# Expert weights of a mixture-of-experts layer: six transfers of 2 MB per expert in place of twelve of 1 MB

## The reference

```
xn = rmsnorm(h)                                  # 1024 x 1024
top-4 of 32 experts per token, softmax gates
per expert e, in blocks of 128 tokens:
    gu = xb @ w_gu[e] + b_gu[e]                  # 1024 -> 2048: g, u
    h  = (clip(u) + 1) * (min(g, 7) * sigmoid(1.702 * min(g, 7)))
    yb = h @ w_down[e] + b_down[e]               # 1024 -> 1024
h = h + sum over the token's 4 experts of gate * y
out = rmsnorm_final(h)
```

## Time and profile before

| | |
|---|---|
| time, median of 3 runs | 2607.06 us (2603.6 to 2607.36) |
| profiled execution | 2609.65 us, its span 2608.0 us |
| TensorE busy | 2352.2 us (90%) |
| VectorE busy | 1590.6 us (61%) |
| ScalarE busy | 1117.3 us (43%) |
| moved by DMA | 514.21 MB |
| expert weight transfers | 256 of w_gu and 128 of w_down, 1 MB each |
| item loop | from about 990 us to about 2518 us |

### The profile page before, as it was taken

The page is one execution under the profiler, slowest core; times in us unless marked ns, Lnnn a source line. Parts: engine busy times, 40 slices in busy tenths (PEclk is TensorE's granted clock), DMA queues, the critical chain, the costliest instruction groups (busy, mean ns, idle before and its releaser), DMA issues.

```text
span 2608.0 us, 31503 instructions
## 1 busy us (share of the span) xinstructions
PE 2352.2 (90%) x9494; PEld 1711.6 (66%) x9495; DVE 1590.6 (61%) x1522; ACT 1117.3 (43%) x1047; POOL 350.5 (13%) x338
## 2 busy tenths in 40 slices
PE   7997499989999956999999999999999999999960
PEld 4553374554554525888888888888888787778840
DVE  4446841110131366786876666787778779978748
ACT  4123120030130213565654544556566567765632
POOL 0370300000000052010110100111011011110016
PEclk9989659989999957999999999999999999999985
DMA  4002010130100116786876866778789789997857
GB/s 151 33 1 83 1 81 33 35 126 29 36 19 1 67 66 235 289 302 222 327 268 225 290 224 211 281 278 324 254 313 369 247 313 370 371 338 267 313 209 289
DMA packets 215265, 514.21 MB, mean 197 GB/s; under 512 B 19140, under 2 KB 19338, under 8 KB 214520
## 3 DMA queue, kind: packets, MB, share of 16 engines
q1 hardware_dynamic: 194912, 450.72, 48.5%
q0 software_dynamic: 18352, 62.60, 6.4%
q10 hardware_dynamic: 1960, 0.35, 0.1%
HBM read 481.97 MB, written 30.48 MB: 196 GB/s over the span
## 4 chain that ended last, share of the span: by engine, by line
PE 44%; issue 5%; DVE 5%; DMA 5%; ACT 2%; POOL 1%; DVEq 1%; ACTq 0%; POOLq 0%; SPq 0%
PE PS L839 17%; PE PS L860 10%; PE PS L843 9%; PE PS L867 5%; DVE WL L1602 2%; DMA WA<-in_exp_w_down 2%; DMA WA<-in_exp_w_gu 2%; PE PS L892 1%; PE PS L831 1%; DVE H L1212 1%; PE PS L804 1%; POOL WA L1884 1%; ACT WH L1112 1%; ACT WH L1117 1%; DVE XEL L1598 0%
## 5 line engine op out<-in xcount | busy, mean ns | idle before, releaser
L1602 DVE TENSOR_TENSOR WL<-WA,WH 128x2048 fp32r<-128x2048 f32 x384 | 876.6, 2290 | 288.4 <-ACT WH L1133 117.8
L839 PE MATMUL PS<-WH,XEL 128*128 128x512 f32 x1344 | 361.1, 391 | 0.0
L839 PE MATMUL PS<-WH,XEH 128*128 128x512 f32 x1344 | 360.7, 390 | 0.0
L843 PE MATMUL PS<-WL,XEH 128*128 128x512 f32 x1344 | 347.6, 390 | 0.0
L1117 ACT CAST WH<-WA 128x2048 fp32r<-128x2048 f32 x128 | 243.9, 1908 | 201.8 <-PE PS L843 150.5
L1112 ACT CAST WH<-WA 128x2048 fp32r<-128x2048 f32 x128 | 244.5, 1910 | 190.4 <-PE PS L843 155.0
L1133 ACT CAST WH<-WA 128x2048 fp32r<-128x2048 f32 x124 | 236.5, 1909 | 199.3 <-PE PS L867 181.8
L839 PEld LDWEIGHTS PS<-WH,XEL 128*128 128x128 f32 x1344 | 253.2, 188 | 53.3
L843 PEld LDWEIGHTS PS<-WL,XEH 128*128 128x128 f32 x1344 | 253.2, 188 | 52.9
L839 PEld LDWEIGHTS PS<-WH,XEH 128*128 128x128 f32 x1344 | 253.1, 188 | 52.1
L538 PE MATMUL PS<-XT,WB 128*128 128x512 f32 x512 | 223.2, 597 | 1.1 <-issue 1.1
(11 more groups left out here) (249 smaller groups left out, 2373.4 us busy)
## 6 DMA issues: line engine op xcount, KB each, us to landing
WA<-in_exp_w_gu SPq DMA_DIRECT2D x256, 1024.0 KB, 6.4
WA<-in_exp_w_down SPq DMA_DIRECT2D x128, 1024.0 KB, 6.1
y_rows<-WA POOLq DMA_DIRECT2D x42, 512.0 KB, 6.7
WB<-in_xa_wkv SPq DMA_DIRECT2D x4, 2048.0 KB, 8.0
WB<-in_w_in SPq DMA_DIRECT2D x3, 2048.0 KB, 10.4
H<-in_x SPq DMA_DIRECT2D x4, 1024.0 KB, 5.9
WB<-in_w_out SPq DMA_DIRECT2D x2, 2048.0 KB, 7.8
WA<-in_x SPq DMA_DIRECT2D x1, 4096.0 KB, 12.2
```

What stands on the lines that cost most here:

```text
L839: nc.tensor.matmul(PS[:, 2 * h + t, :], x[:, KT4 * half + k, t * P:(t + 1) * P], WH[:, j % 4, k * HALF:(k + 1) * HALF], start=False, stop= ...
L843: ins = nc.tensor.matmul(PS[:, 2 * h + t, :], XEH[:, KT4 * half + k, t * P:(t + 1) * P], WL[:, j % 4, k * HALF:(k + 1) * HALF], start=Fals ...
L1602: v.tensor_tensor(WL[:, s, :], RAW[:, s, :], WH[:, s, :].bitcast(F32), sub).then_inc(done, 1)
```

## The change

The slots of the raw ring are filled in pairs: slots 0 and 1 by one transfer of 2 MB, slots 2 and 3 by another. SP waits for the second slot of the pair to be free, instead of each in turn, and the landing semaphores are one per pair, so ScalarE may start on either slot only when both have landed. The conversion by ScalarE and VectorE stays one slot at a time, as do WH, WL and TensorE's work. The pieces within a transfer keep their form: 2 KB contiguous for gate/up, 4 KB for down.

```diff
-            for j in range(4):
-                load_gate_up(j, slice(0, 1))
+            for u in range(2):
+                load_gate_up(u, slice(0, 1))
...
+            def load_gate_up(u, e):
                 f, h = divmod(u, 2)
+                b = u % 2
+                sp.dma_start(RAW[:, 2 * b:2 * b + 2, :].rearrange("p j (k c) -> p (j k) c", k=KT4),
+                             gu_v[:, e, :, h, f, :].rearrange("p e k c -> p (e k) c")).then_inc(rg_in[b], 16)
+
+            def load_down(b, e):
+                sp.dma_start(RAW[:, 2 * b:2 * b + 2, :].rearrange("p j (k d) -> p (j k) d", k=2),
+                             dn_v[:, e, b, :, :].rearrange("p e k d -> p (e k) d")).then_inc(rd_in[b], 16)
...
-                    for s in range(4):
-                        sp.wait_ge(gu_low, 8 * i + s + 1)
-                        load_gate_up(4 + s, bass.ds(e_i, 1))
+                    for b in range(2):
+                        sp.wait_ge(gu_low, 8 * i + 2 * b + 2)
+                        load_gate_up(2 + b, bass.ds(e_i, 1))
...
-                            sp.wait_ge(gu_low, 8 * i + m + 5)
-                            load_down(m, bass.ds(e_p, 1))
+                            sp.wait_ge(gu_low, 8 * i + 2 * b + 6)
+                            load_down(b, bass.ds(e_p, 1))
...
-                            sp.wait_ge(dn_low, 4 * i + s + 5)
-                            load_gate_up(s, bass.ds(e_n, 1))
+                            sp.wait_ge(dn_low, 4 * i + 2 * b + 6)
+                            load_gate_up(b, bass.ds(e_n, 1))
...
-                    act.wait_ge(rg_in[s], 32 * i + 32)
+                    act.wait_ge(rg_in[s // 2], 32 * i + 32)
...
-                    act.wait_ge(rd_in[m], 16 * i)
+                    act.wait_ge(rd_in[m // 2], 16 * i)
...
-                    act.wait_ge(rg_in[s], 32 * i + 48)
+                    act.wait_ge(rg_in[s // 2], 32 * i + 48)
```

More of the change, by code:

```diff
@@ L323, in build @@
         bdn_in, tri_done, fg_in, h3_done = sem("bdn_in"), sem("tri_done"), sem("fg_in"), sem("h3_done")
-        rg_in = [sem(f"raw{s}_gu_in") for s in range(4)]
-        rd_in = [sem(f"raw{s}_dn_in") for s in range(4)]
+        rg_in = [sem(f"raw_pair{s}_gu_in") for s in range(2)]
+        rd_in = [sem(f"raw_pair{s}_dn_in") for s in range(2)]
         gu_high, gu_low, gu_used = sem("gu_high"), sem("gu_low"), sem("gu_used")
@@ L455, in _ @@
             sp.dma_start(BDN[0:E, :], A["exp_b_down"]).then_inc(bdn_in, 16)
[L456 to L461, removed]
+            gu_v = A["exp_w_gu"].rearrange("e (k p) (h f c) -> p e k h f c", p=P, h=2, f=2)
+            dn_v = A["exp_w_down"].rearrange("e (m k p) d -> p e m k d", p=P, k=4)
+            def load_gate_up(u, e):
                 f, h = divmod(u, 2)
[L463 to L469, removed]
+                b = u % 2
[4 more added lines that the diff above has]
+                             dn_v[:, e, b, :, :].rearrange("p e k d -> p (e k) d")).then_inc(rd_in[b], 16)
             wait_filled(sp, ("xt3", L - 1, 1))
             sp.wait_ge(xn_out, 16 * L)
-            for j in range(4):
-                load_gate_up(j, slice(0, 1))
+            for u in range(2):
+                load_gate_up(u, slice(0, 1))
             sp.wait_ge(itm_done, 1)
@@ L487, in _ @@
                     e_i = item_expert(sp, i)
-                    for s in range(4):
-                        sp.wait_ge(gu_low, 8 * i + s + 1)
-                        load_gate_up(4 + s, bass.ds(e_i, 1))
+                    for b in range(2):
+                        sp.wait_ge(gu_low, 8 * i + 2 * b + 2)
+                        load_gate_up(2 + b, bass.ds(e_i, 1))
                 with sp.If_cmp(n_p, 0, "IS_GT"):
                     e_p = entry(sp, 0, i, E - 1)
-                    for m in range(4):
+                    for b in range(2):
                         with sp.If_cmp(n_i, 0, "IS_GT"):
-                            sp.wait_ge(gu_low, 8 * i + m + 5)
-                            load_down(m, bass.ds(e_p, 1))
+                            sp.wait_ge(gu_low, 8 * i + 2 * b + 6)
+                            load_down(b, bass.ds(e_p, 1))
                         with sp.Else():
-                            sp.wait_ge(dn_low, 4 * i + m + 1)
-                            load_down(m, bass.ds(e_p, 1))
+                            sp.wait_ge(dn_low, 4 * i + 2 * b + 2)
+                            load_down(b, bass.ds(e_p, 1))
                 with sp.If_cmp(n_n, 0, "IS_GT"):
@@ L502, in _ @@
                     with sp.If_cmp(n_p, 0, "IS_GT"):
-                        for s in range(4):
-                            sp.wait_ge(dn_low, 4 * i + s + 5)
-                            load_gate_up(s, bass.ds(e_n, 1))
+                        for b in range(2):
+                            sp.wait_ge(dn_low, 4 * i + 2 * b + 6)
+                            load_gate_up(b, bass.ds(e_n, 1))
                     with sp.Else():
-                        for s in range(4):
-                            sp.wait_ge(gu_low, 8 * i + s + 5)
-                            load_gate_up(s, bass.ds(e_n, 1))
+                        for b in range(2):
+                            sp.wait_ge(gu_low, 8 * i + 2 * b + 6)
+                            load_gate_up(b, bass.ds(e_n, 1))
             sp.wait_ge(moe_done, 1)
@@ L1095, in _ @@
             for j in range(4):
-                act.wait_ge(rg_in[j], 16)
+                act.wait_ge(rg_in[j // 2], 16)
                 nc.scalar.copy(WH[:, j, :], RAW[:, j, :]).then_inc(gu_high, 1)
```

## The result

The changed kernel takes 2808.98 us (median of 4, 2802.27 to 2809.98) against 2607.21 before: a ratio of 1.077, 95% interval 1.075 to 1.079. The forecast was 2743 us in a range of 2680 to 2830: slower, as forecast, but by 202 us in place of 136.

The account below looks back on a forecast made before the run. TensorE bounds two-tile turns; in one-tile turns TensorE, VectorE and DMA are about equal and the raw ring has no slack. One-tile stretches lose 157 us, less 21 already lost: +136 on the profiled 2609.65, so 2743 us, range 2680 to 2830.

Parts of the forecast that it names:

- The ring as the bound of one-tile turns: Raw ring of two pairs: a round of 16.1 us, 48.4 us a one-tile turn where TensorE needs 35.3; chance 0.65.
- TensorE's waits: In the one-tile stretch after the change, TensorE was to wait for VectorE's difference at L1602.
- T: Landing time of a 2 MB transfer into the raw ring: 8.6 us, bounds 7.6 and 9.9.
- Two-tile turns hide it: With two tiles the flow takes 4.2 us per slot against TensorE's 5.88, so TensorE stays the bound and turns are unchanged.
- The stock: Slots ready behind a two-tile stretch: eight, worth 8.7 us in one-tile slots; four two-tile slots give 6.7 back.
- Larger transfers are cheaper: Rival: DMA pays its fixed part half as often, one-tile turns fall to TensorE's 35.3 us, total 2586 us; chance 0.04.
- Hidden by the stock: Rival: slots in stock hide the delay in one-tile turns, total 2607 us; chance 0.03.
- The clock: Rival: TensorE's clock falls after each starved pause, about 2 us each, +72 us on top, total 2815; chance 0.12.
- Crowding: Rival: the two pairs' transfers crowd each other, landing near 9.9 us, total 2827 us; chance 0.16.

Follow-up runs that it names:

- e7: Changed kernel with VectorE's hidden step moved ahead of slot 6 and of down slot 2, in one-tile turns alone: 2759.45 us, ratio to before 1.058.
- e1: Kernel before, 1 MB transfers kept, both of a pair issued only when its second slot is free and used only when both landed: 2799.35 us, ratio 1.073.
- e10: Changed kernel with twelve idle matmuls ahead of TensorE's wait for the hidden step in one-tile turns: 2804.26 us, ratio to before 1.075.

## Why the prediction was right in kind and short in size

**The ring as the bound of one-tile turns: right.** Forecast 48.4 us a turn, from a round of 16.1; measured 47.8 to 49.7 in the turns that have one tile throughout (48.7 in the run), rounds 15.4 to 16.2 in the 25th turn. Three parts of the round have an experiment: late asking and late use alone give the turns of their own sums within 1 us, and with the two `hidden` steps of 1.38 us out of it the mean round over six pairs is 16.1 - 2.76 / 6 = 15.6, the turn 46.9; measured 46.9 (e7). TensorE's waits were forecast at the wrong VectorE operation, but what those wait for is the same late pair.

**T: right.** 8.9 in place of 8.6. With 8.9 the sum gives 49.3 a turn, 0.6 over the measured mean, so the other terms are together a little too long.

**Two-tile turns hide it: right**, to 0.1 us.

**The stock: wrong, and here lie the 57 us that the profiled difference of 192.6 has over 136.** The sum took eight slots in stock behind a two-tile stretch and 6.7 us regained by four two-tile slots. By turns, measured increase over before, forecast in brackets:

| turns | increase, us |
|---|---|
| 4, 6, 15, 18, 23, 30 | 40.6 (26.4) |
| 10, 13 | 11.5 (0) |
| 7, 16 | 23.6 (10) |
| 19 to 21 | 30.9 (25.2) |
| 24 to 28 | 55.7 (48.5) |
| 31 to the end | 21.4 (22.5) |
| the first two | 9.0 (3) |

For the 7th and 16th turn and the runs from the 19th and the 24th on the sum had taken off 6.7 us each, 26.8 in all; they lost 26.5 more than forecast. So four two-tile slots gave nothing back there.

The raw ring does not hold four slots ahead. Its second pair can only be asked for when slot 3 of the item has been split, and slot 3 can only be copied when TensorE has used up the last down slot, that is when it starts the turn. The rows of the tenth turn show it: slot 3's copy is released by TensorE's last down slot (L866) at 1481.22; the pair is asked for at 1485.62, 3.8 us after the turn's start at 1481.81; landing 11.3; copy and difference 4.2; `hidden` 1.5. That is 20.8 us, and TensorE is through with slot 5 after 17.3. However long the two-tile stretch was, six slots are in stock and no more.

The same sum with 8.6 for the landing gives 18.1, so a late `hidden` and a longer landing (11.3 in the 7th turn too) each add to it. This pause, 3.57 us, is the larger part of the 5.4 that the tenth turn lost; behind it TensorE ran at the lower clock until 1506.33 and took some 1.6 us longer, and with that clock filled (e10) 1.4 of it came back as a wait on VectorE. By that a gate/up stretch of one tile loses some 6 us whatever went before it (the eight turns of the first two lines: 52.1 / 8 = 6.5), and a whole one-tile turn some 13 us over TensorE's 35.3 to 36.2, whatever it has in stock. For twelve one-tile slots the sum had booked 4.4 behind a full stock and 6.4 behind four two-tile slots.

The six slots were read from the code and these rows; no run changes how far the ring reaches. Nor was it tried by itself what keeps the stock from serving twice, in the 7th and the 16th turn. That 2809 still lies in the range is in part luck: its upper part was there for a T of 9.9 or for the clock, and neither filled it.

**The rivals.** *Larger transfers are cheaper*: out; e1 has the couplings with 1 MB transfers, and beside it 2 MB is if anything some 10 us the dearer (1.077 against 1.073 of before). *Hidden by the stock*: out, as above. *The clock*: its falls came, 0.91 in the run; filling one pause a turn took nothing off the run. *Crowding*: partly there, 11.3 us for the pair 6/7 in the tenth turn, where two stores of 512 KB to `y_rows` are issued 1.6 and 2.8 us behind it; that these are what delays it was not tried.

## What to carry to other kernels

A ring's round is landing plus everything up to the last release; joining two slots adds the second slot's work to the round and halves the number of rounds in flight, and here, from 512 KB to 2 MB, the size of the transfer hardly mattered beside it. Before joining, compare the round with what the consumer takes for one ring of slots: here 11.5 against 11.8 us, no slack, so that the joined round of 16.1 was felt in full; with two tiles the joined round is 16.8 against 23.5, and the same change was free. And count a stock of slots by what must have happened before each can be asked for, not by the number of buffers: here slot 3 could not be prepared before TensorE had finished the turn before, and a step one place late in VectorE's order made the wait longer.

## What the runs showed that was not expected

The couplings are more than additive: 52 and 75 us alone, 191 together. Splitting 1 MB into two of 512 KB cost 10 us over 384 slots, 0.03 us each. And moving a VectorE step that waits for TensorE one place ahead cost 1.4 to 1.7 us in most turns that open with two tiles, and gained up to 4.4 us in one-tile turns of the changed kernel: one written order does not suit both kinds of turn.
